# Latent tokens by grid columns, and a 192- or 256-key window for each query tile of neighbourhood attention

## The reference, cut to what matters

```python
def _neighbourhood_attention(q, k, v, k_ctx, v_ctx, rpb):
    rows = L // GRID_W                                   # 512 // 64 = 8
    kr, kc = min(NA_ROWS, rows), NA_COLS                 # 8, 16
    r0 = jnp.clip(r - kr // 2, 0, rows - kr)
    c0 = jnp.clip(cidx - kc // 2, 0, GRID_W - kc)
    in_win = (cidx[None, :] >= c0[:, None]) & (cidx[None, :] < c0[:, None] + kc)
    bias = rpb[:, dr[:, None, :, None], dc[None, :, None, :]]
    s_win = einsum('brchd,brmnhd->bhrcmn', qg, kg) * scale + bias[None]
    s_win = jnp.where(in_win[None, None, None, :, None, :], s_win, -jnp.inf)
    s_ctx = einsum('brchd,bkhd->bhrck', qg, k_ctx) * scale
    p = softmax(concatenate([s_win, s_ctx], axis=-1))
    return (einsum('bhrcmn,brmnhd->brchd', p_win, vg)
            + einsum('bhrck,bkhd->brchd', p_ctx, v_ctx))
```

## Time and profile before

| | us |
|---|---|
| median of three runs | 3356.33 |
| lowest, highest | 3352.59, 3363.98 |
| span of the profiled execution | 3358.8 |
| PE busy in it | 3259.7 (97%) |
| DVE busy | 1475.8 (44%) |
| ACT busy | 904.0 (27%) |
| POOL busy | 287.4 (9%) |
| values for attention (L1353), 690.0 to 716.3 | 26.3 |
| 40 units of neighbourhood attention, 719.5 to 843.1 | 123.6 |
| 40 units of latent attention, 918.1 to 1025.3 | 107.2 |

### The profile page before, as it was taken

One profiled execution on the slowest core, in us unless ns is written; L12 is line 12 of the kernel. 1 busy time (PEld: TensorE's weight loads), 2 busy tenths in 40 slices (PEclk: granted clock), 3 DMA queues, 4 the chain that ended last, 5 costly groups with the idle time before them and its releaser, 6 DMA issues.

```text
span 3358.8 us, 49554 instructions
## 1 busy us (share of the span) xinstructions
PE 3259.7 (97%) x20192; PEld 3002.8 (89%) x20192; DVE 1475.8 (44%) x2057; ACT 904.0 (27%) x1278; POOL 287.4 (9%) x365
## 2 busy tenths in 40 slices
PE   8999999999999999999999999999999999999999
PEld 5999999976879999999999999868687786999999
DVE  3564634257554655624652524343342434422223
ACT  3112113235354211214212214222222222322222
POOL 1000001012001000001000001030200203000001
PEclk8999999999999999999999999999999999999999
DMA  8443422221101443422442222212122121122221
GB/s 202 155 157 113 150 65 73 81 70 23 59 1 64 145 151 119 161 76 68 147 149 75 94 69 72 96 38 85 54 82 69 44 88 38 57 81 70 77 73 69
DMA packets 84778, 299.37 MB, mean 89 GB/s; under 512 B 10384, under 2 KB 12720, under 8 KB 83985
## 3 DMA queue, kind: packets, MB, share of 16 engines
q1 hardware_dynamic: 57888, 206.77, 18.3%
q0 software_dynamic: 20560, 73.84, 8.0%
q10 hardware_dynamic: 6176, 16.54, 1.4%
HBM read 289.62 MB, written 8.44 MB: 89 GB/s over the span
## 4 chain that ended last, share of the span: by engine, by line
PE 89%; DVE 3%; issue 2%; ACT 2%; DMA 2%; POOL 1%; SPq 0%; ACTq 0%; DVEq 0%; POOLq 0%
PE ps L1177 37%; PE ps L1160 29%; PE ps L1353 11%; PE ps L1407 2%; PE ps L1202 2%; PE ps L1382 2%; PE ps L1568 1%; PE ps L1559 1%; ACT tmp_g L486 1%; DMA ada<-in_ada 1%; PE ps L1395 1%; PE ps L1547 1%; PE ps L1210 1%; DMA mhalf<-in_mhalf 1%; PE ps L1215 1%
## 5 line engine op out<-in xcount | busy, mean ns | idle before, releaser
L1177 PE MATMUL ps<-h,w 128*128 128x320 f32 x8928 | 1339.5, 312 | 26.9 <-DVE w L764 10.8
L1177 PEld LDWEIGHTS ps<-h,w 128*128 128x128 f32 x8928 | 1326.1, 190 | 35.3 <-issue 13.0
L1160 PE MATMUL ps<-g,w 128*128 128x320 f32 x5376 | 809.4, 312 | 5.8 <-DVE g L1123 5.8
L1160 PEld LDWEIGHTS ps<-g,w 128*128 128x128 f32 x5376 | 801.5, 191 | 7.7 <-issue 7.7
L764 DVE TENSOR_TENSOR w<-raw,w 128x1024 fp32r<-128x1024 f32 x383 | 459.4, 1221 | 281.6 <-ACT w L461 277.4
L461 ACT ACTIVATE w<-raw 128x1024 fp32r<-128x1024 f32 x207 | 216.2, 1061 | 607.6 <-PE ps L1160 473.3
L1353 PE MATMUL ps<-w,h 128*128 128x512 f32 x1596 | 367.9, 391 | 5.1 <-ACT rv L708 3.1
L1353 PEld LDWEIGHTS ps<-w,h 128*128 128x128 f32 x1596 | 298.1, 188 | 68.5 <-issue 4.7
L859 DVE TENSOR_TENSOR tmp_g<-tmp_s,ps 128x640 f32<-128x640 f32 x88 | 72.3, 822 | 603.4 <-ACT tmp_s L502 603.4
L502 ACT ACTIVATE tmp_s<-ps 128x640 f32<-128x640 f32 x88 | 62.1, 706 | 903.3 <-PE ps L1177 903.3
L782 DVE SCALAR_TENSOR_TENSOR acc<-ada,sc,acc 128x1024 f32<-128x1024 f32 x224 | 273.8, 1280 | 1.5 <-DMA ada<-in_ada 1.5
(11 more groups left out here) (160 smaller groups left out, 1982.0 us busy)
## 6 DMA issues: line engine op xcount, KB each, us to landing
raw<-in_ws SPq DMA_DIRECT2D x383, 512.0 KB, 3.7
ada<-in_ada POOLq DMA_DIRECT2D x132, 512.0 KB, 4.0
ada<-in_ada ACTq DMA_DIRECT2D x6, 1024.0 KB, 17.0
rst<-in_state ACTq DMA_DIRECT2D x4, 1024.0 KB, 4.9
out_new_state<-rsx ACTq DMA_DIRECT2D x8, 512.0 KB, 2.6
bias<-rp_rep POOLq DMA_DIRECT2D x16, 224.0 KB, 4.3
x<-in_xT SPq DMA_DIRECT2D x1, 2560.0 KB, 25.9
rp_rep<-in_rpb POOLq DMA_DIRECT2D x1, 930.0 KB, 37.0
```

What stands on the lines that cost most here:

```text
L1160: mm = pe.matmul(pair_half(pr, half, width), w2[:, slot, wi, at:at + cols], rhs(k, ri)[:, half * width:(half + 1) * width], start=(k == 0 ...
L1177: mm = pe.matmul(pair_half(pr, half), w2[:, n % RING, wi, k * P:(k + 1) * P], h2[:, k, ri, half * HT:(half + 1) * HT], start=(k == 0 and w ...
```

## The change

The latent tokens are laid out column by column of the grid (token = 8 x column + row), so a tile of 128 queries is 16 whole columns, and the keys that it can see are one contiguous piece: 192 keys for the first and last tile, 256 for the two in the middle. Everything in the layers before the retention mixer works in this order.

- **Scores**: a latent unit has a matmul of 192 or 256 columns and the one of 128 cached keys, written side by side; one DVE instruction scales and adds the bias for both (the bias tile has zeros for the cached part), in place of two.
- **Softmax**: maximum, exponential and product run over 320 or 384 columns, not 640.
- **Transposes and values**: three in a latent unit, not five; the copy between them takes 384 columns, not 640.
- **Value tiles**: windows don't start at multiples of 128, so six token tiles are formed (start columns in `V_AT`), with two that are used by halves; 144 matmuls, and six copies on ACT.
- **Bias**: the host lays out one contiguous 128 x 256 tile for each head. POOL loads it with one DMA and adds the mask in three instructions (192, 256 and 192 columns) into a tile of 1024 columns. The scratch tensor, its DMA `rp_rep` and the 16 gathers are gone. Once at the start POOL clears six pieces of 128 columns.
- **Retention**: it needs row order. `norm` before it lets ACT read the latent part by columns (a step of 8 elements) and write it by rows; in the retention heads `add_to_x` reads and writes `x` with a step of 8 elements.
- Rotation tables follow the new order; latent attention and the FFNs have the same instructions as before.

```diff
-V_BANK = [2, 3, 4, 5, 0]
+V_BANK = [2, 3, 4, 5, 0, 1]
+V_AT = [0, NCTX, NCTX + 64, NCTX + 192, NCTX + 320, NCTX + 384]
+NA_WINDOW = {1: (0, 192), 2: (64, 256), 3: (192, 256), 4: (320, 192)}
+NA_CHUNKS = {1: [(0, 0, 0, P), (64, 1, 64, P), (192, 4, 0, P)],
+             2: [(0, 1, 0, P), (128, 2, 0, P), (256, 4, 0, P)], ...
...
-            pool.dma_start(a["rp_rep"].rearrange("r (e w) -> r e w", w=RPW),
-                           a["rpb"].rearrange(...).to_broadcast([NAH * RPR, RP_REP, RPW])).then_inc(rp_rep, 16)
             ada_loop(2 * KD, 8 * 8)
...
-                for r2 in range(2):
-                    src = bass.AP(a["rp_rep"].tensor, ...)
-                    pool.dma_start(bias[64 * r2:64 * r2 + 64, h % 2, :]..., src).then_inc(bias_ld[h % 2], 16)
-                pool.tensor_tensor(b3, b3, colmask..., ALU.add).then_inc(bias_rdy, 1)
+                for b, n0, n1, m0 in ((1, 8, 32, 0), (2, 0, 32, 24), (4, 0, 24, 56)):
+                    dst = bias[h % 2][:, NA_BIAS[b]:NA_BIAS[b] + n * ROWS]...
+                    ins = pool.tensor_tensor(dst, r3[:, n0:n1, :], colmask[...]..., ALU.add)
+                ins.then_inc(bias_rdy, 1)
...
-                    for part, st in ((ctx_of, 0), (lat_of, 1)):
+                    for st in range(2):
+                        if nn == RET_NORM and st:
+                            dst, src = by_rows(dst), by_columns(src)
+                        ins = act.activation(dst, src, ACT.Identity, ...)
...
+                    if rows and st:
+                        dst, src = by_columns(dst), by_rows(src)
+                    ins = dve.scalar_tensor_tensor(dst, src, g[:, m, st:st + 1], dst, ALU.mult, ALU.add)
...
-                    dve.scalar_tensor_tensor(sbs[g % 3][:, 0:NLAT], src[:, 0:NLAT], NAD ** -0.5,
-                                             bias[:, h % 2, at:at + NLAT], ALU.mult, ALU.add)
-                    link(dve.tensor_scalar(sbs[g % 3][:, NLAT:T], src[:, NLAT:T], NAD ** -0.5, None, ALU.mult))
-                    dve.tensor_reduce(nm, sbs[g % 3], AX.X, ALU.max, negate=True).then_inc(s_neg, 1)
+                    nk, at = keys_of(b, na), NA_BIAS[b]
+                    link(dve.scalar_tensor_tensor(sbs[g % 3][:, 0:nk], src[:, 0:nk], NAD ** -0.5,
+                                                  bias[h % 2][:, at:at + nk], ALU.mult, ALU.add))
+                    dve.tensor_reduce(nm, sbs[g % 3][:, 0:nk], AX.X, ALU.max, negate=True).then_inc(s_neg, 1)
...
-            tok_tiles(n0 + 14, 4, of_h, KD, range(NT), lambda t: V_BANK[t], v_wait)
+            tok_tiles(n0 + 14, 4, of_h, KD, range(len(V_AT)), lambda t: V_BANK[t], v_wait,
+                      lambda ap, t: ap[:, V_AT[t]:V_AT[t] + P])
...
-                    pe.matmul(ps[:, 2 * (g % 2), :], lhs, lat_of(k[:, PAST:]), ...)
-                    mm = pe.matmul(ps[:, 2 * (g % 2) + 1, 0:P], lhs, k[:, 0:PAST], start=True, stop=True)
+                    pe.matmul(sc_out[:, 0:nw], lhs, lat_of(k[:, PAST:])[:, w0:w0 + nw], start=True, stop=True)
+                    mm = pe.matmul(sc_out[:, nw:nw + PAST], lhs, k[:, 0:PAST], start=True, stop=True)
...
+                if b and na:
+                    for kt, (_, tile, k0, k1) in enumerate(NA_CHUNKS[b]):
+                        mm = pe.matmul(ps[r0:r0 + 64, 6, (b - 1) * P:b * P], va[k0:k1, tile, h * 64:h * 64 + 64],
+                                       pt[k0:k1, kt, (b - 1) * P:b * P], start=(kt == 0), stop=(kt == 2))
```

More of the change, by code:

```diff
@@ L165, in build @@
         ka = over("ka", 4 * (PAST + T), ada_at).rearrange("p (k t) -> p k t", k=4)
-        bias = over("bias", 2 * 14 * GRID_W, ada_at).rearrange("p (a c) -> p a c", a=2)
+        bias0 = over("bias0", NA_BIAS_COLS, ada_at)
+        rows = over("rows", 2 * NA_SPAN, ada_at).rearrange("p (a c) -> p a c", a=2)
+        el[0] += 1024
         esq = place("esq", 2 * T, at=el[0]).rearrange("p (a t) -> p a t", a=2)
@@ L566, in _ @@
             act.dma_start(va[:, 4, :], a["cache_v"]).then_inc(em_ld3, 16)
[L567 to L570, removed]
+            for t in range(len(V_AT)):
+                act.activation(va_ctx if t == 0 else va[:, V_OF[t], :], ps[:, V_BANK[t], :], ACT.Copy
+                               ).then_inc(v_ev, 1)
+            act.wait_ge(v_ev, 1)
+            act.dma_start(a["new_v"], va_ctx).then_inc(out_done, 16)
             act.wait_ge(em_kr, 1)
@@ L827, in norm, with add_to_x @@
                                           h2[:, k - 1, 0, :].bitcast(fp32), ALU.subtract).then_inc(h_lo, 1)
-            def add_to_x(m, pr, g, count):
+            def add_to_x(m, pr, g, count, rows=False):
                 if count > 8:
                     dve.wait_ge(x_upd, count - 8)
-                for part, st in ((ctx_of, 0), (lat_of, 1)):
-                    ins = dve.scalar_tensor_tensor(part(x[:, m, :]), part(pair(pr)),
-                                                   g[:, m, st:st + 1], part(x[:, m, :]), ALU.mult, ALU.add)
+                for st in range(2):
+                    dst, src = ((ctx_of, lat_of)[st](u) for u in (x[:, m, :], pair(pr)))
+                    if rows and st:
+                        dst, src = by_columns(dst), by_rows(src)
+                    ins = dve.scalar_tensor_tensor(dst, src, g[:, m, st:st + 1], dst, ALU.mult, ALU.add)
                 ins.then_inc(x_upd, 1)
@@ L1426, in _ @@
             pe.wait_ge(em_ld3, 16)
-            pe.wait_ge(v_ev, NT)
+            pe.wait_ge(v_ev, len(V_AT))
             pe.wait_ge(c_n, 5)
@@ L1689, in shape_constants @@
     c["rope_ret"] = r.reshape(P, -1)
-    ci = np.arange(GRID_W)
-    c0 = np.clip(ci - NA_COLS // 2, 0, GRID_W - NA_COLS)
-    win = (ci[None] >= c0[:, None]) & (ci[None] < c0[:, None] + NA_COLS)
-    c["colmask"] = np.tile(np.where(win, 0.0, NEG).astype(f), (2, 1))
+    q = (np.arange(P) // ROWS)[:, None]
+    ends = [(np.maximum(q - 8, 0), 24), (q, 32), (np.minimum(q, 8), 24)]
+    wins = [(np.arange(n)[None] >= lo) & (np.arange(n)[None] < lo + NA_COLS) for lo, n in ends]
+    c["colmask"] = np.where(np.concatenate(wins, 1), 0.0, NEG).astype(f)
     i, j = np.arange(P)[None, :], np.arange(P)[:, None]
@@ L1708, in shape_constants, with bias_rows @@
     return c
+def bias_rows(rpb):
+    wide = np.pad(rpb, ((0, 0), (0, 0), (8, 8)))
+    out = np.empty((NAH, 16, ROWS, 32, ROWS), np.float32)
+    for c in range(16):
+        for r in range(ROWS):
+            out[:, c, r] = wide[:, NA_ROWS - 1 - r:2 * NA_ROWS - 1 - r, 15 - c:47 - c].transpose(0, 2, 1)
+    return out.reshape(NAH, P, NA_SPAN)
 def columns(v):
```

107 lines of the change are left out of this document (66 added, 41 removed).

## The result

The changed kernel takes 3374.61 us (median of four runs, 3370.11 to 3381.07), the kernel before 3359.18 us in runs beside it (3352.59 to 3363.98). The ratio is 1.0053, with a 95% interval of 1.0035 to 1.0071: half a per cent slower, where 1.1% faster was forecast. The profiled execution's span is 3371.7 us against 3358.8, and its mean granted clock 0.963 against 0.978.

The account below looks back on a forecast made before the run. PE work and the few places where PE waits were taken to bound the kernel. Terms -37.6 (units) + 6.0 (value projection) - 9.0 (first FFN) + 4 (retention) = -36.6 us: median 3356.3 to 3320 us, 8-in-10 range 3308 to 3337.

Parts of the forecast that it names:

- I put the loss at 5 us, not 7: Start of the attention units, after the value copies: low clock there costs 5 us, where it cost about 7 before.
- so I let it stay high: Attention units after their start: PE busy 69 of 81 us, 0.85, so the clock was taken to stay high.
- The comparison with 746 to 752 us: Attention units before the change: a stretch 5.00 of 6.00 busy at clock 1.00, used as evidence the clock stays high.
- The clock rival: Attention units: clock stays at 1.2 GHz, stage 115 us, sum -7.6 us, 3349 us; chance 9%.
- The units at full clock: Attention units: 8.6 us PE work a head, 69 for eight, plus 12 waits and 5 clock: 86 us, 37.6 less.
- DVE did not become the bound: Rival, attention units: DVE becomes the bound, stage about 97 us, sum -25.6 us, 3331 us; chance 18%.
- POOL's bias additions: Attention units: POOL's additions stop DVE, 0 to 1.3 us in each of six heads, taken as 0.7: 4.2 us.
- The value projection: Ahead of the units: 24 more matmuls, 5.45 us, and a sixth ACT copy, 0.5 us: 6.0 us more.
- The first FFN: First loop: without the scratch DMA delaying the ada load, 9.0 us less; ends 7.65 and 9.8.
- The retention steps: Retention layer: accesses stepping by 8 elements cost 0 to 8.3 us; the middle taken, 4 us more.
- The end "doubles the time": Retention layer: the step doubles a 512-column piece's time, 4.0 us on ACT and 4.3 on DVE, 8.3 in all.
- The slower rival by this mechanism: Rival, retention layer: steps make the kernel slower from 2.5 us extra a piece; at 3 us, 3364 us; chance 3%.

Follow-up runs that it names:

- the run at 1.00: Changed kernel with the value blocks of latent units done twice in heads 0 and 1 alone: 3333.0 us, ratio 0.9923, units 96.8 us.
- the kernel with the opening: Changed kernel with six identity matmuls before the transposes of each of the first five units, no gap fill: 3329.09 us, ratio 0.9911; again 3330.51 us.
- the fill in the gap together with the opening: Changed kernel with 16 identity matmuls before the first score and six before the transposes of each of the first five units: median 3350.03 us, ratio 0.9964.
- the gap filled: Changed kernel with 16 identity matmuls between value projection and first score, while ACT copies the values: 3374.25 us, ratio 1.004, units 135.9 us.
- the kernel without steps: Changed kernel without its reordering around the retention mixer (RET_NORM = -1, rows=False): 3364.84 us, ratio to the kernel before 1.0017.

## Why the prediction was wrong, by its own steps

**The clock (wrong, and it decides).** The failing step is "I put the loss at 5 us, not 7", and "so I let it stay high" behind it. I took the rise after 13.1 us as a property of the stage that stays when its units change, and asked only whether a high clock would be kept. The trace of before does not show what lifted it. The runs do: in the changed kernel it never rose in 138 us; with more PE work in each latent unit it rose at 736 to 746 us (in nine of twelve executions, by time and mean clock, where only half of these units had more), with more in the first two heads at 734 us, and with work in the opening 7 us into the units. The thin units, one behind the other, did not lift the clock, though the same units mostly keep a high one. The comparison with 746 to 752 us, 5.00 of 6.00 busy, could speak only for the keeping.

**The clock rival (right mechanism, mis-sized, under-weighted).** It gave 115 us for the stage and 3349 us. It came true with 138.5 and 3374.6. The term that was mis-sized most is the value block at the low clock: I took 1.79 us for ten records at the low clock against 1.23 at the high one, a factor of 1.45, from the block at 731.60 to 733.39. That block straddles the clock's rise at about 732.6, so it is a mixture. Six records take 1.47 (748.56 - 747.09) in the changed kernel at 0.50, and 0.80 (789.38 - 788.58) in the run at 1.00, a factor of 1.84. The rival had 1.07 for them; the missing 0.40 us are 13 us over 32 latent units, of 24 in all. The rest is work that was sized low before any factor: at 0.50 the window scores took 0.80 and 1.02 us where the rival had 0.76 on average, the three transposes 0.83 for 0.76, and the context unit more too. With a head of 17.41 us the rival's stage is 139 us, 15 us above the stage before, and its sum 15 + 6.0 - 9.0 + 4 = +16: slower, not "within 0.3%". (Twice the head of 8.6 us would also give 138, by luck: 8.6 is short, and the measured factors are 1.7 to 1.9.) I had given it 9% and put it on the wrong side. The rise was visible in the very rows that I priced from. The Trainium skill, "TensorE: Matmul & The Clock Gate", HAM oscillation, was cited for this rival with waits between bursts as its mechanism. The trace doesn't agree with that part here: at 0.50 PE was busy for 136.33 of 136.60 us, and 0.3 us of waits are nothing to blame.

**The units at full clock (right, by two errors that cancel).** Forecast 8.6 us of work and 1.5 of waits for each head, 10.1; the run with two doubled heads shows 10.17 and 10.45. The work was sized low: W, V, S of a latent unit with 256 keys took 0.48, 0.80 and 0.53 + 0.31 us (788.10 to 790.22), 2.12 us against 1.95 by the forecast's own terms. The waits were sized high: 69.50 - 66.92 = 2.6 us in the time of nearly seven heads, about 0.4 a head, where the forecast had 1.5. DVE's four instructions of a latent unit took 1.67 us at the mean (0.52, 0.52, 0.15 and 0.47) for 1.64. So DVE did not become the bound, and POOL's bias additions can't have cost more than these 0.4 us a head. The kernel with the opening takes 91.8 us, and its thirty added matmuls are about 9 us of that on PE.

**The value projection (right).** +5.9 us for +6.0, the gap 3.73 us for 3.7.

**The first FFN (right, a little low).** -10.7 us over the loop for -9.0, and -10.3 with that DMA moved alone. (The forecast's 49.31 took its end from the chain and its start from PE's rows; by PE's rows alone it is 49.15, and the forecast 8.8.) The second FFN, taken as the model, has itself an idle PE ahead of this stretch (1.88 us) and did not have the full clock in it. Its stretch before the change, and the loop of the first FFN after it:

```profile
1088.00:1127.00 39.00, 39.00 (x259) 39.00 (x258) 28.93 (x27) 12.00 (x13) 4.33 (x8) 0.96 0.51 166
```

```profile
62.70:115.80 53.10, 53.10 (x363) 52.91 (x362) 41.23 (x42) 22.62 (x32) 4.22 (x8) 1.00 0.42 131
```

0.04 of 39 us is 1.6 us, about what I missed.

**The retention steps (mis-sized).** I took the middle, 4 us. Undone alone they give 7.7 to 9.8 us in the median and 10.0 in the stage; by rows it is 8 x 0.55 on ACT and 8 x 0.50 on DVE, 8.4 us. The two profiles, before and after, have 5.9 between them because single profiles of this stage scatter by 4 us: it took 791.2, 792.1 and 795.4 us in the three profiles of the kernel before and its variants, 791.3 without the steps, and 801.2 to 805.1 in the ten with the steps. The end "doubles the time" was worked out as 8.3 and was the right one. The Trainium skill, "SBUF — State Buffer", Specifications (TRN2), says that a line of 16 bytes gives full bandwidth only at two accesses or more; the trace agrees in kind, with 0.80 become 1.35 us on ACT and 0.74 become 1.24 us on DVE. Splitting the difference between a rule that speaks up and a trace that is silent was no reasoning. The slower rival by this mechanism (2.5 us extra for each piece) was far off.

With the clock as it was in the kernel with the opening, the terms are -32 for the units (their added matmuls in them), +5.9, -10.7 and +8 to 10: -27 to -29 us, and -28 and -27 measured in its two sets of runs. The sum stands apart from the term that I took for granted.

**What stays open.** Why the fill in the gap together with the opening leads, by time and mean clock, to falls in seven of twelve executions, while the opening alone had none in ten, is not settled: both run the same units with the same kind of waits. Nor is it settled what of a thin unit counts for the clock. One thing in the traces bears on it and was not tested: with the gap filled and in the kernel without steps the clock came back 2.2 and 1.5 us ahead of the projection, where the score matmuls have ended and transposes and value matmuls follow each other. Nor is it known why latent attention loses the clock for part of its first 12 us in five profiles of fourteen.

## What to carry to other kernels

On a kernel bound by PE, ask for each shortened stage whether the remaining work will lift the clock again once it has fallen, and price the whole stage at both levels: a busy share of 99.8% says only that PE does not wait. A price at the low clock is taken from a row that lies wholly inside a low stretch. And where a stage starts behind an idle PE, dense matmuls in its first few units are a cheap thing to try, run often enough to see whether the kernel has a second course; a DMA of many small pieces is kept off a queue whose next load is on the path.

## What the hardware did that I had not expected

- The granted clock stayed at 0.50 for 136.60 us while PE was busy for 136.33 of them. Six more value records in each latent unit brought it up and made the stage 23 us shorter (138.5 to 115.5).
- The same instructions ran through at 1.00 in one kernel and at 0.50 in another, and kernels in between took either course from one execution to the next: 3339 to 3357 or 3397 to 3401 us, and 3327 to 3371 us in three groups. Such a kernel has a spread of 1.3 to 1.9%; the mean clock of its executions goes with their time (0.982 at 3327 us, 0.967 at 3371 us).
- Doubled transposes lifted the clock as doubled value matmuls did, though later (746 against 736 us).
- A step of 8 float32 elements in the latent part costs about 0.5 us for 512 columns on either engine: on ACT, which reads with the step, and on DVE, which reads and writes `x` with it.
